# Two early stages of the third mixer in two parts each, other gate arithmetic, fewer and other filler matmuls

## The chip, the cores and the metric

One NeuronCore of a Trainium2 chip runs one program. The metric is the device time of one execution in microseconds. The engines are TensorE (PE, matmuls), VectorE (DVE), ScalarE (ACT), GpSimd (POOL) and the DMA queues that SyncE and ScalarE issue. Each engine works through its own list of instructions in order; semaphores join the lists.

## The reference, cut to what matters

Two layers of a decoder trunk, 512 prompt tokens and 8 sample tokens together (520 columns), width 1024. Each layer has four mixers that share one input projection, four gates, an output projection and a gated feed-forward part:

```python
h = _rmsnorm(x, p['norm_mix_w']) * (1.0 + sc1) + sh1
proj = (h @ p['w_in']).astype(f32)             # columns of the four mixers and of the gates
...
conv = jax.nn.silu(conv)                       # third mixer: 4-tap convolution over tokens
q = _l2norm(_heads(conv[..., :o1], GDN_H)) * HEAD_DIM ** -0.5
k = _l2norm(_heads(conv[..., o1:o2], GDN_H))
g_log = -jnp.exp(p['gdn_a_log']) * jax.nn.softplus(Pg[..., a_off:a_off + GDN_H] + p['gdn_dt_bias'])
beta = jax.nn.sigmoid(Pg[..., a_off + GDN_H:])
o, s_gdn = _gated_delta_chunked(q, k, v, g_log, beta, st_gdn.astype(f32))
...
gates = jax.nn.sigmoid(proj[..., OFF_GATE:])
for n, y_b in enumerate((y_rw, y_ret, y_gdn, y_hg)):
    term = gates[..., n * D_MODEL:(n + 1) * D_MODEL] * (y_b @ p['w_branch'][n])
    merged = term if merged is None else merged + term
out = merged.astype(h.dtype) @ p['w_out']
```

## The kernel before

All four engines walk the same list, made by `plan_layer()`. It interleaves two kinds of entries. The **mixer stages** `("mix", n, i)` are short steps of the recurrences, in the order HG, RW, GD, RT (HGRN2, RWKV-7, gated DeltaNet, retention): each mixer is a Python generator on each engine, and one `yield` ends one stage there. The **dense tasks** are the large products: `proj` (a 128-column tile of the input projection), `gate` (such a tile of a gate's projection, and then the branch product that it gates), `ada` and `turn` (the modulation). `IDLE`, made of the lists `BEFORE`, `PAIR` and `AFTER`, has one number per stage, and the dense tasks are shared out among the stages in proportion to it; its length is the number of stages.

On PE a dense task is a generator too. `operands()` of a stage first runs up to 30 matmuls of the current or next dense task (`fill`), then waits for the stage's operands. A dense entry of the plan makes PE finish that task (`finish`). Only one task beyond those due may be begun. A projection or gate tile is 48 matmuls at L803 (three for each of 8 slices of K and each half of the columns: the weights are split into a rounded part `w_hi` and a rest `ring_lo`); a gate adds four matmuls at L837. Results go to two banks of PSUM, `gm`, in turn. `bank()` waits until the bank's last content was taken: by ACT (L1585 copies a projection, L1594 takes the gate's sigmoid into `GT`, L1333 takes `ada`) or by DVE (L2274 and L2277 multiply branch product and gate, L2220 takes `turn`). Since these takers stand in the list at their place in the plan, a gate is taken only after all that ACT has in the stages before it.

`keep_busy(n)` issues n filler matmuls of constants (L767) whose result nobody reads. They are emitted only where a bank is open to write to. The numbers `AT_START`, `AT_TILE`, `AT_SAMPLES`, `AT_FFN_NORM`, `AT_END` and the arguments `busy=` say how many stand where. The trace shows every 4-byte matmul (L767, L931, L837) as two records, so 22 fillers are 44 records.

The rounding of a weight tile to `w_hi` is done by ACT (L1355) or by POOL (L732), by the set `on_scalar`; the rest `ring_lo` is made by POOL (L735). `early()` is the head of the GD mixer, run during RW: ACT makes six scaled copies of the projections (L1509), and DVE's generator `convolution()` adds the taps; `beside()` runs one or two of its steps inside the RW pair and chunk stages. A pair stage of RW on DVE (L2079 to L2085) calls `beside(2)` first, then takes PE's scores.

In GD the stages 0 and 1 hold, on PE, two sums over heads (L931 on `WK`) and two products of the gate parameters (L931 on `AB`); on ACT the sigmoid, logarithms and exponentials L1521 to L1529; on DVE L2111 to L2128. Stage 2 is the cumulative sum on DVE (L1768, L1774) and three exponentials on ACT (L1534 to L1536). Stage 3 makes the operands L2134 to L2138 on DVE and turns them over on PE (L942).

## Time and profile before

| | |
|---|---|
| Time, median of 3 runs | 2695.78 us (2693.8 to 2711.17) |
| Profiled execution, its time | 2704.68 us |
| Profiled execution, its span | 2702.9 us |
| Mean granted clock of TensorE | 0.928 |
| PE busy | 2361.5 us, 87% of the span |
| DVE, POOL and ACT busy | 1138.1, 844.8 and 731.2 us |
| DMA | 233.39 MB, 86 GB/s |

The span is what the trace covers; the profiled execution's own time is 1.8 us longer, and 8.9 us above the median. The granted clock is a share of TensorE's full speed of 2.4 GHz: 1.00 is 2.4 GHz and 0.50 is 1.2 GHz. The first layer's mixers run from about 45 to 860 us of the span, its feed-forward part to about 1370 us, and the second layer repeats this some 1330 us later.

### The profile page before, as it was taken

The page shows a single profiled execution, that of the slowest core. Times are in us where ns is not written, and L with a number is a line of the kernel's source. Part 1 is how long each engine was busy: PE and PEld are TensorE (multiplying, and loading weights), DVE is VectorE, ACT ScalarE, POOL GpSimd, SP SyncE. Part 2 cuts the span into 40 slices and gives each one's busy share as a digit, 9 for nine tenths or more (in the row PEclk, how much of TensorE's full clock was granted, in tenths as well). Part 3 has the DMA queues.
Part 4 walks back from the last instruction along what each step waited for, and adds up shares of the span by engine and source line. Part 5 has one row for each costly group of instructions (what it writes and reads, how often), then busy time and mean ns, then how long its engine had stood idle before and what let it go on. Part 6 is the DMA issues. An engine that isn't in the chain of part 4 may idle for free. (4 is left out here: it accounts for less than half of the span.)

```text
span 2702.9 us, 46568 instructions
## 1 busy us (share of the span) xinstructions
PE 2361.5 (87%) x20592; PEld 2176.8 (81%) x20592; DVE 1138.1 (42%) x1558; ACT 731.2 (27%) x915; POOL 844.8 (31%) x602
## 2 busy tenths in 40 slices
PE   5878978689899989999977789777898899999997
PEld 3767866578778979999976679656787699999997
DVE  5164464555444532221233546655734445222212
ACT  2432311322212232222224333104222133322222
POOL 2311210133133434444432213101322234444442
PEclk8988988889999999999988989778999999999998
DMA  6331121111232324322233311111112322222222
GB/s 250 118 110 57 60 72 46 45 51 45 80 102 87 117 88 127 120 91 87 94 120 117 105 54 59 61 55 48 52 52 73 115 77 102 79 94 94 87 93 73
DMA packets 68457, 233.39 MB, mean 86 GB/s; under 512 B 10784, under 2 KB 11296, under 8 KB 67872
## 3 DMA queue, kind: packets, MB, share of 16 engines
q1 hardware_dynamic: 61344, 214.88, 24.1%
q10 hardware_dynamic: 6912, 15.53, 1.6%
q8 instruction: 162, 2.65, 0.4%
q14 instruction: 39, 0.32, 0.0%
HBM read 219.03 MB, written 11.35 MB: 85 GB/s over the span
## 5 line engine op out<-in xcount | busy, mean ns | idle before, releaser
L735 POOL TENSOR_TENSOR ring_lo<-ring,w_hi 128x512 fp32r<-128x512 f32 x552 | 769.9, 1416 | 1429.8 <-ACT w_hi L1355 1361.2
L803 PE MATMUL gm<-H_hi,ring_lo 128*128 128x260 f32 x3456 | 749.2, 299 | 98.1 <-ACT GT L1594 34.1
L803 PE MATMUL gm<-H_hi,w_hi 128*128 128x260 f32 x3456 | 720.9, 290 | 0.0
L803 PE MATMUL gm<-H_lo,w_hi 128*128 128x260 f32 x3456 | 719.9, 291 | 0.0
L803 PEld LDWEIGHTS gm<-H_hi,ring_lo 128*128 128x128 f32 x3456 | 559.6, 197 | 142.5 <-ACT GT L1594 39.9
L803 PEld LDWEIGHTS gm<-H_lo,w_hi 128*128 128x128 f32 x3456 | 554.2, 196 | 2.3 <-issue 1.9
L803 PEld LDWEIGHTS gm<-H_hi,w_hi 128*128 128x128 f32 x3456 | 553.7, 195 | 1.6 <-issue 0.8
L1355 ACT ACTIVATE w_hi<-ring 128x1024 fp32r<-128x1024 f32 x268 | 282.9, 1056 | 447.4 <-PE gm L803 186.0
L752 POOL TENSOR_TENSOR X<-X,GT 128x520 f32<-128x520 f32 x32 | 49.8, 1557 | 323.6 <-DVE GT L2277 323.6
L1279 PE MATMUL gm<-AF_hi,ring_lo 128*128 128x260 f32 x704 | 142.1, 283 | 3.3 <-DVE AF_lo L2301 3.3
L1279 PE MATMUL gm<-AF_hi,w_hi 128*128 128x260 f32 x704 | 141.5, 282 | 0.0
L1279 PE MATMUL gm<-AF_lo,w_hi 128*128 128x260 f32 x704 | 141.3, 282 | 0.0
L2306 DVE TENSOR_TENSOR AT<-gm,GT 128x520 f32<-128x520 f32 x44 | 30.8, 700 | 253.0 <-ACT GT L1635 253.0
L2235 DVE TENSOR_SCALAR Y<-gm,MOD 128x520 f32<-128x520 f32 x32 | 24.3, 759 | 258.0 <-PE gm L1279 217.1
L1594 ACT ACTIVATE GT<-gm 128x520 f32<-128x520 f32 x64 | 38.6, 603 | 343.7 <-PE gm L803 316.5
L837 PE MATMUL gm<-Y,WB 128*128 128x260 f32 x512 | 123.6, 384 | 0.0
L1279 PEld LDWEIGHTS gm<-AF_hi,ring_lo 128*128 128x128 f32 x704 | 108.3, 188 | 3.7 <-DVE AF_lo L2301 3.7
L1279 PEld LDWEIGHTS gm<-AF_lo,w_hi 128*128 128x128 f32 x704 | 108.6, 188 | 0.0
L1279 PEld LDWEIGHTS gm<-AF_hi,w_hi 128*128 128x128 f32 x704 | 108.3, 188 | 0.0
L767 PE MATMUL gm<-CN 128*128 128x128 f32 x652 | 86.9, 296 | 21.6 <-ACT PJ L1585 13.5
L767 PEld LDWEIGHTS gm<-CN 128*128 128x128 f32 x652 | 83.7, 210 | 24.4 <-ACT PJ L1585 15.5
L837 PEld LDWEIGHTS gm<-Y,WB 128*128 128x128 f32 x512 | 93.4, 191 | 11.6
(410 smaller groups left out, 2750.4 us busy)
## 6 DMA issues: line engine op xcount, KB each, us to landing
ring<-wall SPq DMA_DIRECT2D x372, 512.0 KB, 3.3
WB<-wbranch SPq DMA_DIRECT2D x32, 256.0 KB, 3.6
xsave<-X SPq DMA_DIRECT2D x2, 2080.0 KB, 12.1
X<-xsave ACTq DMA_DIRECT2D x8, 520.0 KB, 5.3
arena<-states ACTq DMA_DIRECT2D x8, 512.0 KB, 3.4
sst<-arena ACTq DMA_DIRECT2D x8, 512.0 KB, 3.7
X<-xt SPq DMA_DIRECT2D x1, 2080.0 KB, 12.1
y<-H SPq DMA_DIRECT2D x4, 520.0 KB, 2.7
```

Of the source, the lines that this page charges most:

```text
L735: pool.tensor_tensor(ring_lo[:, SLOT[i], k], ring[:, SLOT[i], k], hi[:, k].bitcast(F32), ALU.subtract).then_inc(parts_ready, 1)
L752: pool.tensor_tensor(MG[:, m, :], MG[:, m, :], GT[:, :], ALU.add).then_inc(gate_used, 1)
L767: pe.matmul(out, cst("blocks"), cst("ident"), start=False, stop=False, skip_group_check=True)
L803: ins = pe.matmul(out[:, hf, 0:HALF], w[a][:, k, :], src[b][:, k, HALF * hf:HALF * (hf + 1)], start=first and a == "lo", stop=last and a == b)
L837: ins = pe.matmul(out[:, hf, 0:HALF], WB[:, m // 2 % 2, m % 2, k, :], Y[:, k, HALF * hf:HALF * (hf + 1)], start=k == 0, stop=k == 1)
L1279: ins = pe.matmul(out[:, hf, 0:HALF], w[a][:, i % 8, :], AF_parts[b][:, f, HALF * hf:HALF * (hf + 1)], start=f == 0 and a == "lo", stop=f ...
L1355: act.activation(w_hi[:, j % 2], ring[:, SLOT[splits[j][0]]], ACT.Copy).then_inc(hi_made, 1)
L1594: act.activation(h2(GT[:, :]), src, ACT.Sigmoid).then_inc(done, 1)
L2235: step(ts(h2(WR), src, MOD[:, at + m, 0:1], None, MUL))
L2306: taken(tt(h2(AT[:, f % 2, :]), src, h2(GT[:, :]), MUL), done)
```

## The change

There are seven edits.

1. **GD stages in two.** `BEFORE[GD]` has two entries more, and each engine's generator has its `yield`s to match. Old stage 0 (both head sums, with all of L1521 to L1529 on ACT) becomes stages 0 and 1, with gate task RW 0 between them in the plan; old stages 1 and 2 move to 2 and 3, and old stage 2's exponentials on ACT go to stage 4, behind gate task RW 2.
2. **Gate arithmetic.** ACT takes tanh(x/2) where it took the sigmoid. DVE computes (tanh + 1) times the product in one instruction, and the factor 0.5 goes into the split of the merged sum.
3. **Convolution later.** `convolution()` begins with two empty steps, so the first `beside(2)` does nothing.
4. **Fillers at tiles.** `AT_TILE` and `AT_SAMPLES` have other numbers. In each layer 12 fillers fewer stand ahead of projection tile GD 2, 7 fewer at GD 5, 15 fewer at RT 1, 3 fewer at RT 6 and 2 fewer at gate GD 0; 5 more at gate RW 7, 8 more at HG's sample stage, 4 more at the start.
5. **Fillers ahead of a bank wait.** `AT_BANK` puts 18 fillers ahead of the waits of `ada` 18 and of projection RW 2 (`("proj", 1, 2)`), 12 ahead of that of projection GD 0; they write to the unused half of a bank (`half_only`).
6. **Feed-forward norm.** 18 fillers instead of 22 in the first layer, 26 in the second. The arguments `busy=21` and `busy=4` of RW's pair stages go; no bank is open at those places, and the instruction lists have no filler there before or after.
7. **Rounding moved.** With `BUSY` and `held_up`, nine tiles of each layer are rounded by POOL (L732) that were rounded by ACT (L1355).

```diff
-AT_START, AT_END, AT_FFN_NORM, AT_INNER = 14, 6, 22, 7
-AT_TILE = {("proj", 2, 2): 20, ("proj", 2, 5): 7, ("proj", 3, 1): 15, ("proj", 3, 6): 8, ("gate", 2, 0): 7}
-AT_SAMPLES = {0: (0, 0), 1: (22, 5), 2: (0, 5), 3: (2, 0)}
+AT_START, AT_END, AT_INNER, AT_SUMS, AT_FFN_NORM = 18, 6, 7, (0, 22), (18, 26)
+AT_TILE = {("proj", 2, 2): 8, ("proj", 3, 6): 5, ("gate", 2, 0): 5, ("gate", 1, 7): 5}
+AT_BANK = {("ada", 0, 18): 18, ("proj", 1, 2): 18, ("proj", 2, 0): 12}
+AT_SAMPLES = {0: (8, 0), 1: (22, 5), 2: (0, 5), 3: (0, 0)}
...
-          GD: [10, 10, 8, 8, 4] + [5] * DIAGONAL,
+          GD: [8, 2, 10, 4, 4, 8, 4] + [5] * DIAGONAL,
...
+BUSY = {(RW, 3), (RW, 4), (RW, 6), (GD, 1), (GD, 5), (GD, 7), (GD, len(BEFORE[GD])), (GD, len(BEFORE[GD]) + 6), (RT, 0)}
...
+            held_up = {j for j in range(3, mixing + 2)
+                       if any(kind == "mix" and (n, m) in BUSY for kind, n, m in plan[at[j - 3]:at[j - 2]])}
...
+                    if (kind, n, m) in AT_BANK and any(half_only):
+                        keep_busy(AT_BANK[kind, n, m], gm[:, half_only.index(True), 1, HALF:HALF + P128])
...
-                        act.activation(h2(GT[:, :]), src, ACT.Sigmoid).then_inc(done, 1)
+                        act.activation(h2(GT[:, :]), src, ACT.Tanh, scale=0.5).then_inc(done, 1)
...
                 def convolution():
 
+                    yield
+                    yield
                     from_scalar()
...
-                            taken(tt(h2(GT[:, :]), src, h2(GT[:, :]), MUL), done)
+                            taken(stt(h2(GT[:, :]), h2(GT[:, :]), 1.0, src, ADD, MUL), done)
```

**PE, start of GD.** The list from the last part of gate RW 0 to the second product of `AB` (L837 is the branch product of a gate, L931 on `arena` a head sum; a line of dots stands for further rows of the same tile). Before:

```order
L837 MATMUL gm<-Y,WB 128x260 x4
L931 MATMUL mx<-arena,CN 128x260 x4
L803 MATMUL gm<-H_hi,ring_lo 128x260 x2
...
L931 MATMUL mx<-AB,CN 128x260 x4
L803 MATMUL gm<-H_hi,ring_lo 128x260 x2
...
L837 MATMUL gm<-Y,WB 128x260 x4
L931 MATMUL mx<-AB,CN 128x260 x4
```

After (lines 808, 842 and 940 are 803, 837 and 931 of before):

```order
L842 MATMUL gm<-Y,WB 128x260 x4
L808 MATMUL gm<-H_hi,ring_lo 128x260 x2
...
L940 MATMUL mx<-arena,CN 128x260 x4
L808 MATMUL gm<-H_hi,ring_lo 128x260 x2
...
L842 MATMUL gm<-Y,WB 128x260 x4
L940 MATMUL mx<-AB,CN 128x260 x8
```

Thirty matmuls of gate RW 1 now stand ahead of the second head sum, and the other eighteen with its branch product behind it; between the two products of `AB` nothing stands any more, where before 18 matmuls and a branch product did.

**ACT, start of GD.** The same stretch (L1525 is the logarithm of a head sum, L1527 the exponentials, L1594 a gate, L1534 the exponentials of old stage 2). Before:

```order
L1525 ACTIVATE arena<-mx,CN 128x1040 x2
L1527 ACT_TABLE_LOAD
L1527 ACTIVATE arena<-arena 128x1040 x2
L1528 ACTIVATE arena<-arena 4x520
L1529 ACT_TABLE_LOAD
L1529 ACTIVATE arena<-arena,CN 4x520
L1594 ACT_TABLE_LOAD
L1594 ACTIVATE GT<-gm 128x520
...
L1534 ACT_TABLE_LOAD
L1534 ACTIVATE DI<-arena 128x16
```

After (L1535 is 1525, L1539 is 1527, L1541 is 1529, L1607 is 1594, L1547 is 1534):

```order
L1535 ACTIVATE arena<-mx,CN 128x1040
L1607 ACT_TABLE_LOAD
L1607 ACTIVATE GT<-gm 128x520
...
L1535 ACT_TABLE_LOAD
L1535 ACTIVATE arena<-mx,CN 128x1040
L1539 ACT_TABLE_LOAD
...
L1541 ACTIVATE arena<-arena,CN 4x520
L1607 ACT_TABLE_LOAD
L1607 ACTIVATE GT<-gm 128x520 x2
...
L1547 ACTIVATE DI<-arena 128x16
```

Gate RW 0 is taken between the two logarithms, gates RW 1 and RW 2 both before the exponentials of L1534, and those need no table load of their own. Over the program there are 68 table loads instead of 74; one new load in each layer stands ahead of L1514, the sigmoids of the convolution.

**DVE, first pair stage of RW.** Before:

```order
L1724 COPY CVO<-PJ 128x6x8
L1698 TENSOR_TENSOR CT<-CVI,PR 128x48 x2
...
L2079 TENSOR_TENSOR arena<-mx,CN 128x1024
L2080 TENSOR_TENSOR arena<-mx,CN 128x1024
L1709 SCALAR_TENSOR_TENSOR PJ<-PJ,PR 128x509
L1709 SCALAR_TENSOR_TENSOR PJ<-PJ,PR 128x510
L2084 TENSOR_TENSOR arena<-mx,CN 128x1024
```

After (L2094, L2095 and L2099 are 2079, 2080 and 2084; L1713 is 1698):

```order
L1739 COPY CVO<-PJ 128x6x8
L2094 TENSOR_TENSOR arena<-mx,CN 128x1024
L2095 TENSOR_TENSOR arena<-mx,CN 128x1024
L1713 TENSOR_TENSOR CT<-CVI,PR 128x48 x2
...
L1718 TENSOR_TENSOR arena<-arena,CT 128x2x8
L2099 TENSOR_TENSOR arena<-mx,CN 128x1024
```

The two scores are taken ahead of the convolution's first step, which waits for ACT's six copies; the last two additions of the convolution (L1709) now come behind L1908, after RW's sample stages.

## Rows read from the trace of the kernel before

**Rows 1.** The page, busy time by engine.

```profile
PE 2361.5 (87%) x20592; PEld 2176.8 (81%) x20592; DVE 1138.1 (42%) x1558; ACT 731.2 (27%) x915; POOL 844.8 (31%) x602
```

**Rows 2.** Who PE waited for: total us, times, longest us.

```profile
PE gm L803 <- ACT GT L1594: 34.1, 6, 9.4
...
PE mx L955 <- DVE arena L2080: 21.1, 4, 8.2
...
PE gm L803 <- DVE MT L2220: 14.3, 2, 7.2
...
PE gm L803 <- ACT PJ L1585: 10.0, 2, 5.0
```

**Rows 3.** Timeline, first pair stage of RW, first layer (start us, us).

```profile
376.30 0.19 DVE L1724 COPY CVO<-PJ 128x48 f32<-128x48 f32 x1
...
381.59 0.45 DVE L1698 TENSOR_TENSOR CT<-CVI,PR 128x48 f32<-128x48 f32 x2 [5.10 <-ACT arena L1509]
...
384.57 1.21 DVE L2080 TENSOR_TENSOR arena<-mx,CN 128x1024 f32<-128x1024 f32 x1
...
385.83 2.08 PE L955 MATMUL mx<-arena,PJ 64*128 64x128 f32 x16 [7.85 <-DVE arena L2080]
...
392.15 0.69 PE L998 MATMUL mx<-arena 32*32 32x32 f32 x32 [0.66 <-DVE arena L2085]
```

**Rows 4.** Timeline, start of GD, first layer.

```profile
518.83 2.02 PE L931 MATMUL mx<-arena,CN 128*128 128x260 f32 x8 [2.54 <-DVE arena L2112]
...
526.60 1.13 ACT L1525 ACTIVATE arena<-mx,CN 128x1040 f32<-128x1040 f32 x1 [2.19 <-PE mx L931]
527.74 1.28 ACT L1527 ACT_TABLE_LOAD   x1
529.04 2.17 ACT L1527 ACTIVATE arena<-arena 128x1040 f32<-128x1040 f32 x2
...
535.88 0.80 PE L803 MATMUL gm<-H_hi,ring_lo 128*128 128x260 f32 x2 [9.38 <-ACT GT L1594]
...
542.37 2.02 PE L931 MATMUL mx<-AB,CN 4*128 4x260 f32 x8
...
561.50 1.23 DVE L1774 TENSOR_TENSOR arena<-arena 128x1024 f32<-128x1024 f32 x1
...
567.11 0.80 PE L803 MATMUL gm<-H_hi,ring_lo 128*128 128x260 f32 x2 [7.38 <-ACT GT L1594]
...
568.09 2.21 DVE L2135 TENSOR_TENSOR arena<-PJ,arena 128x1024 f32<-128x1024 f32 x1
...
569.18 4.48 POOL L735 TENSOR_TENSOR ring_lo<-ring,w_hi 128x512 fp32r<-128x512 f32 x2
...
573.73 1.23 DVE L2138 TENSOR_TENSOR arena<-PJ,arena 128x1024 f32<-128x1024 f32 x1
```

**Rows 5.** Stretches: length; PE, PEld, DVE, ACT, POOL busy; granted clock; DMA.

```profile
536.00:542.00 6.00, 6.00 (x28) 6.00 (x29) 2.71 (x3) 0.78 (x1) 4.46 (x3) 0.51 0.01 3
...
567.00:572.00 5.00, 4.89 (x22) 4.89 (x23) 4.75 (x4) 1.01 (x2) 4.07 (x3) 0.50 0.00 0
...
239.00:245.00 6.00, 5.83 (x27) 5.84 (x28) 0.00 (x0) 2.34 (x3) 2.50 (x2) 0.50 0.06 11
```

**Rows 6.** Timeline, fillers of the first layer, by start.

```profile
290.81 1.83 PE L767 MATMUL gm<-CN 128*128 128x128 f32 x14 [1.00 <-ACT PJ L1585]
...
511.22 5.07 PE L767 MATMUL gm<-CN 128*128 128x128 f32 x44
...
626.83 5.24 PE L767 MATMUL gm<-CN 128*128 128x128 f32 x30 [2.48 <-DVE GT L2277]
...
628.09 2.50 POOL L735 TENSOR_TENSOR ring_lo<-ring,w_hi 128x512 fp32r<-128x512 f32 x2
```

**Rows 7.** POOL's groups by shape: count, busy us, mean ns.

```profile
L732 POOL TENSOR_TENSOR w_hi<-ring,CN 128x1024 fp32r<-128x1024 f32 x8 | 16.4, 2046 | 15.9 <-DMA ring<-wall 14.2 <-PE gm L803 1.7
```

**Rows 8.** Timeline, ACT at the end of RW, first layer.

```profile
497.69 2.17 ACT L1514 ACTIVATE PJ<-PJ 128x1040 f32<-128x1040 f32 x2 [24.06 <-issue]
```

More of the change, by code:

```diff
@@ L656, in build @@
                 room_after[i] = latest
-            on_scalar = {j for j, (i, _) in enumerate(splits)
-                         if j >= mixing + 2 and j - mixing - KT not in (0, 1) or (2 <= j < mixing + 2 and room_after[i] <= at[j - 2])}
+            held_up = {j for j in range(3, mixing + 2)
+                       if any(kind == "mix" and (n, m) in BUSY for kind, n, m in plan[at[j - 3]:at[j - 2]])}
+            on_scalar = {j for j, (i, _) in enumerate(splits) if j not in held_up
+                         and (j >= mixing + 2 and j - mixing - KT not in (0, 1)
+                              or (2 <= j < mixing + 2 and room_after[i] <= at[j - 2]))}
             rounds_after = {at[j - 2]: j in on_scalar for j in range(2, mixing + 2)}
@@ L847, in ada @@
                     out = bank()
+                    half_only[(used[1] - 1) % 2] = True
                     for k in range(0, KT // 2, 2):
@@ L863, in turn @@
                     out = bank()
+                    half_only[(used[1] - 1) % 2] = True
                     for h in range(2):
@@ L986, in diagonal_scores, with inverse @@
                     return ins
-                def inverse(cp, busy=0):
+                def inverse(cp):
                     def blocks():
@@ L994, in blocks @@
                                 yield u, u // 2 * NC + 2 * cp + u % 2, slice(a, a + BLK), slice(a + BLK, a + 2 * BLK)
-                    operands(FILL_SHORT, busy=busy)
+                    operands(FILL_SHORT)
                     for u, m, i, j in blocks():
@@ L1144, in rwkv @@
                         yield
-                        operands(busy=4 if cp else 21)
+                        operands()
                         scores(0, cp, pj(RW, 1), WK[:, 0])
@@ L1148, in rwkv @@
                         yield
-                        yield from inverse(cp, 4 if cp else 0)
+                        yield from inverse(cp)
                         for ci in range(2):
@@ L1256, in _ @@
                 coming(-1)
-                if layer + 1 == DEPTH:
-                    keep_busy(AT_FFN_NORM, mx[:, 3, 0:P128])
+                keep_busy(AT_SUMS[layer], mx[:, 3, 0:P128])
                 pe.wait_ge(operands_v, count.next(operands_v))
                 feature_sums()
-                keep_busy(AT_FFN_NORM, mx[:, 3, 0:P128])
+                keep_busy(AT_FFN_NORM[layer], mx[:, 3, 0:P128])
                 for m in range(2 * FT):
@@ L1593, in _ @@
                         gates += 1
-                        act.activation(h2(GT[:, :]), src, ACT.Sigmoid).then_inc(done, 1)
+                        act.activation(h2(GT[:, :]), src, ACT.Tanh, scale=0.5).then_inc(done, 1)
                         g[0] += 1
                         if n == RT and m:
-                            step(act.activation(MG_hi[:, m - 1, :], MG[:, m - 1, :], ACT.Copy), for_vector)
+                            step(act.activation(MG_hi[:, m - 1, :], MG[:, m - 1, :], ACT.Copy, scale=0.5), for_vector)
                     if x in rounds_after and rounds_after[x]:
@@ L1600, in _ @@
                 act.wait_ge(gate_used, gates)
-                step(act.activation(MG_hi[:, KT - 1, :], MG[:, KT - 1, :], ACT.Copy), for_vector)
+                step(act.activation(MG_hi[:, KT - 1, :], MG[:, KT - 1, :], ACT.Copy, scale=0.5), for_vector)
                 for k in range(0, KT, 2):
@@ L2114, in gdn @@
                     projected(GD)
+                    yield
                     from_scalar()
@@ L2228, in split_sum @@
                     from_scalar()
-                    step(tt(MG_lo[:, m, :], MG[:, m, :], MG_hi[:, m, :].bitcast(F32), SUB), x_ready)
+                    step(stt(MG_lo[:, m, :], MG[:, m, :], 0.5, MG_hi[:, m, :].bitcast(F32), MUL, SUB), x_ready)
                 def residual(m, at):
@@ L2273, in _ @@
                             dve.wait_ge(x_saved, 16)
-                            taken(tt(h2(MG[:, m, :]), src, h2(GT[:, :]), MUL), done)
+                            taken(stt(h2(MG[:, m, :]), h2(GT[:, :]), 1.0, src, ADD, MUL), done)
                             step(dve.tensor_copy(NA[:, :], NA[:, :]), gate_used)
                         else:
-                            taken(tt(h2(GT[:, :]), src, h2(GT[:, :]), MUL), done)
+                            taken(stt(h2(GT[:, :]), h2(GT[:, :]), 1.0, src, ADD, MUL), done)
                             if n == RT:
```

10 lines of the change are left out of this document (8 added, 2 removed).

## The prediction

> **What bounds the kernel now.** I read the page's busy times first: PE works 2361.5 of 2702.9 us [rows 1], no other engine half of it. So the 341 us in which PE stands, and the stretches at half clock, are what a change of order can win. The list of waits then says whom PE waits for [rows 2]: first for ACT taking a gate (34.1 us in 6 waits), and high up for DVE's L2080 (21.1 us in 4). The timeline shows the two large ones of each kind, once per layer. In GD's first stage PE stands 9.38 us until ACT, after two logarithms, the exponentials and their table loads, takes gate RW 0; behind the next stage it stands 7.38 us, since gate RW 1's successor is taken only after the exponentials of L1534 [rows 4]. In RW's first pair stage PE stands 7.85 us because DVE's L2079 and L2080 stand behind a convolution step that waits for ACT's copies [rows 3]. After such waits the granted clock is at its lower level for some us: 0.51 over 536 to 542, 0.50 over 567 to 572 [rows 5]. The reader is to see in each that the engine named did other work first: order, not speed, makes the wait.
>
> **The change part by part, for one layer.**
>
> *A, convolution later.* DVE is through with L1724 at 376.5, and PE's scores are there (PE ended them before it finished gate HG 4). L2079 and L2080, 1.2 us each, then end at 379.0 instead of 385.8 [rows 3]. PE goes on at 379.0 and needs 2.1 us at full clock for the scores. DVE's next pair, L2084 and L2085, stands behind the convolution's step, which ACT still releases at 381.6; its small products take 1.8 us, the pair 2.4: ready at 385.8. PE's L998 starts there at 392.15 [rows 3]. So of the 7.85 us, 6.3 are won, and a new wait of some 3 us ahead of L998 is what is late next. The two additions pushed behind RW's samples cost DVE 0.75 us each, once, ahead of the next head sum; PE had no wait there, so I put down 1.0. A: -6.3 + 1.0.
>
> *B, GD in two.* I follow the chain from 518.83, where PE starts the first head sum [rows 4]. ACT ends the first logarithm at 524.4 (its next wait, 2.19, begins there), loads a table (1.28), takes gate RW 0 at 526.3. PE, done with that gate at 524.8, waits 1.5 us where it waited 9.38, runs 30 matmuls of gate RW 1 (a fraction of the 48 of a tile, which take 5.8 us at full clock; 3.6), then the second head sum, to 532.0. ACT had the logarithm's input at 526.6 before and has it at 532.0 now: 5.4 us later. From there, 1.13 for the logarithm, 1.28, 2.17 and 0.64 for load and exponentials, 1.28 and 0.73 for the last logarithm: 539.2; DVE's two steps on `AB` end at 540.5. PE starts the first product of `AB` there, 1.8 us ahead of 542.37 [rows 4], after standing some 4 us. The second follows with only DVE's copy between (1.24): 544.0 where it was 550.0. From there to the end of L1774 it took 12.7 us before, so DVE ends at 556.8 instead of 562.7. Then ACT's exponentials (2.3) and, with gate RW 2 already taken, no table load, no gate and no further product on DVE ahead of L2134: 559.3 against 567.9. DVE's five steps to L2138 took 7.1 us, with POOL beside them (2.21 for L2135, against 1.23 for L2138 of the same size [rows 4]); I keep 6.5. PE turns them over at about 565.8 instead of 575.0: -9.2, and it can be -11 if POOL is elsewhere. PE has 11.3 us of dense work between 546 and there, so it stands about 7 us just ahead of L942, and the clock falls as it did. The cover of the chain is gone, the chain is the bound of this stretch; behind it the lists are alike. The bounds are 0 (the chain stays as long as it was) and -11. B: -9.2.
>
> *C, fillers.* 22 fillers, 44 records, take 5.07 us [rows 6]: 0.23 each at full clock. At GD 2 twelve go, but PE next waits for a chain of DVE (token shifts) that ends where PE arrives now: 0. At GD 5 the 7 take 1.83 and a wait for the tile's rest stands behind them, which POOL's own rounding removes: -2.4. At RT 1 the 15 take 5.24, partly at the lower clock [rows 6]; they start at 626.83, POOL's L735 for that tile starts at 628.09 and has its first half by 629.35, so PE goes on at 629.4 instead of 631.8: -2.4. The 3 and 2 others: -1.2. The 5 added at gate RW 7 lie in the 2.48 us ahead of 626.83: 0. C: -6.0.
>
> *D, fillers ahead of bank waits.* 18, 18 and 12 fillers are 4.1, 4.1 and 2.8 us; the waits are 6.5, 7.2 and 5.0, the last two standing in [rows 2] as two equal waits each (14.3 and 10.0). They are covered. What they can give is clock: PE worked 5.83 us of 239 to 245 at the lower level [rows 5], half of it is 2.9. Whether it is given I can't see; bounds 0 and -6 for the three places; I take -1.5.
>
> *E, table load at L1514.* ACT goes straight from a sigmoid gate to L1514 now [rows 8]; behind tanh a load of 1.28 stands in between, and what follows (gate HG 7, L2097 on DVE behind it, the next head sum) is a chain: +1.3. This trace has the next instruction right behind a load: 527.74 plus 1.28 is 529.02, and L1527 starts at 529.04 [rows 4]. The Trainium skill (ScalarE: Activation LUTs, "What ACT_TABLE_LOAD costs") adds a drain of 1380 ns to each switch; by it E would be +2.7 and the whole 3 us later, and the trace doesn't bear it out.
>
> *F, rounding on POOL.* 2.05 us a tile [rows 7] against 1.05 on ACT. POOL is busy 31% of the span [rows 1] and the tile is needed a dense task (5.8 us) later: covered. Not free is its company: L2135 takes 1.0 longer beside POOL [rows 4]. One of the nine in DVE's bound stretch: +1.0; bounds 0 and the rival's. DVE's fused gate product against a plain one: equal in the trace's instructions of this shape within 0.1, and DVE isn't the bound at most of them: 0. Fillers at the start, at HG's samples and at the norms stand ahead of waits as long as they: 0.
>
> **Sum.** -5.3 - 9.2 - 6.0 - 1.5 + 1.3 + 1.0 = -19.7 a layer; the second layer's waits are the first's within 0.4 us ([rows 2] has them in pairs), so -39.4. The profiled execution would take 2704.7 - 39.4 = 2665.3; it lies 8.9 above the median of the three, so the median becomes 2656.4. I say **2657**.
>
> **The rivals.**
>
> *R1, the clock pays for the fillers.* 39 fillers of each layer go where they followed a wait, and B leaves waits of 4 and 7 us. For it: every long wait here ends in a stretch at 0.5 [rows 5]. Against: fillers behind a wait run at the low clock themselves, and real matmuls follow at once. One more fall costs half of 4.9 us; at four places a layer, 8 times 2.4 is 19.6: 2676. The Trainium skill (TensorE: Matmul & The Clock Gate, Part 1) says that the default state is throttled and activity releases it; by it the order of filler and work doesn't matter, but the idle time does, and that speaks for this rival at B's waits.
>
> *R2, the split gives back.* The second head sum stands behind 30 matmuls, and a chain that is cut has more hand-overs. If the chain after the second product of `AB` doesn't shorten as I have it, only the 1.8 us of the first product are left: 7.4 less a layer, 2672. That is also the case in which the change doesn't do what it says.
>
> *R3, slower: POOL's rounding.* A tile comes 1.0 us later by the longer rounding and 2.0 later where DVE's company stretches L735 (4.48 for the two beside L2135 [rows 4], 2.50 for two others [rows 6]), and DVE loses 2.05: 5.05 in all where both lie on the path. It decides from 8 of the 18 tiles, where 39.4 is used up; at 10 it is +50.5 and 2707. Against it: PE's waits for POOL are short, and DVE waits for others in most of the stages chosen.
>
> *R4, more.* The clock stays up where the waits shrink: at five places a layer half of some 4 us, 2 each, 20 in all: 2637.
>
> **How the numbers follow.** Forecast 0.48, R1 0.14, R2 0.17, R3 0.07, R4 0.14. The 27 us that are 1% of the median are about what a measurement can tell from no change; the border is 2668.8. The forecast's own spread (0 to -11 of B, 0 to -6 of D, twice) is 2640 to 2675, nine tenths below the border. Faster by over 1%: 0.43 and R4 0.14, a third of R2 and a fifth of R1, 0.66. Slower by over 1%: 0.06, most of R3. Within 1%: 0.28. The range leaves out R3 and the lower part of R4: 2634 to 2684.
>
> **What would show it.** Right: L2080's waits gone, 3 us ahead of L998; the 9.4 us wait at 1 to 2, 4 to 5 us ahead of the first product of `AB`, some 7 ahead of L942; L942 9 us earlier after the first head sum; 626.8's fillers gone with 2.5 us for POOL. Wrong: a mean granted clock below 0.92 (R1), L942 less than 4 us earlier (R2), waits of 3 us or more for `ring_lo` (R3). I would be most wrong if PE, freed at one place, only waits longer for DVE at the next, since these stretches are chains of DVE and ACT.

## The result and the profile after

The changed kernel took 2683.83 us (median of 8 runs, 2675.61 to 2688.24), the kernel before 2702.12 beside it (8 runs): a ratio of 0.9928, interval 0.9906 to 0.9949, or 19.5 us less where 39.4 were forecast. The 2683.83 stand against 2657 and lie at the upper end of the range, 2684. The spans of the two profiled executions, 2702.9 and 2679.4 us, differ by 23.5. On the median of 2695.78 that the prediction started from, the ratio gives 2676.4.

Line numbers moved (x9, x11, x12, x13 and x17 add two more to those of ACT and DVE): L803 is L808 now, L767 is L772, L931 is L940, L942 is L951, L955 is L964, L998 is L1007, L732 and L735 are L737 and L740, L1514 is L1524, L1768 is L1783. Page of the changed kernel, busy time [rows 1], and then its waits of PE [rows 2]:

```profile
PE 2371.0 (88%) x20696; PEld 2188.1 (82%) x20696; DVE 1140.4 (43%) x1558; ACT 706.7 (26%) x891; POOL 880.6 (33%) x620
```

```profile
PE mx L1083 <- DVE arena L1911: 21.3, 8, 6.6
PE gm L808 <- POOL ring_lo L740: 20.9, 10, 5.2
...
PE mx L951 <- DVE arena L2155: 14.5, 2, 7.6
...
PE mx L1007 <- DVE arena L2100: 10.2, 4, 2.6
...
PE mx L940 <- DVE AB L2137: 9.6, 2, 4.8
```

The two waits that the change was aimed at are gone from the head of the list: 34.1 us for ACT's gates and 21.1 us for L2080 [rows 2]. In their place stand waits that were not there: 4.8 us ahead of each first product of `AB`, about 7 ahead of each turning L951, 2.6 ahead of L1007, and 5.2 for `ring_lo`. The timeline of PE shows where they lie. First RW's first pair stage, where 392.15 stood in [rows 3]:

```profile
378.46 0.98 PE L1007 MATMUL mx<-arena 32*32 32x32 f32 x32 [2.60 <-DVE arena L2100]
```

Then the start of GD [rows 4], dense matmuls left out:

```profile
505.27 3.52 PE L940 MATMUL mx<-arena,CN 128*128 128x260 f32 x8 [2.32 <-DVE arena L2127]
516.96 1.92 PE L940 MATMUL mx<-arena,CN 128*128 128x260 f32 x8
527.59 3.83 PE L940 MATMUL mx<-AB,CN 4*128 4x260 f32 x8 [4.82 <-DVE AB L2137]
532.82 3.83 PE L940 MATMUL mx<-AB,CN 4*128 4x260 f32 x8 [1.40 <-DVE arena L2139]
557.45 3.68 PE L951 MATMUL mx<-CN,arena 128*128 128x128 f32 x16 [6.90 <-DVE arena L2155]
```

The reader is to look at the second column, the time an instruction group took. A product over `AB` takes 3.83 us, and took 2.02 in [rows 4]; the turning takes 3.68, and took 1.97 in the kernel before. The windows say why (length, busy us of PE, PEld, DVE, ACT, POOL, granted clock, DMA):

```profile
526.00:530.00 4.00, 2.41 (x6) 1.90 (x7) 1.18 (x3) 2.12 (x3) 0.00 (x0) 0.50 0.00 0
530.00:534.00 4.00, 2.60 (x7) 1.56 (x6) 1.24 (x1) 0.00 (x0) 0.00 (x0) 0.50 0.00 0
534.00:538.00 4.00, 4.00 (x13) 2.93 (x12) 1.24 (x1) 0.00 (x0) 0.00 (x0) 0.50 0.02 4
...
553.00:557.00 4.00, 0.00 (x0) 0.00 (x0) 3.90 (x4) 0.00 (x0) 0.58 (x1) 0.50 0.00 0
557.00:561.00 4.00, 3.55 (x17) 3.55 (x18) 0.40 (x1) 0.00 (x0) 0.00 (x0) 0.50 0.00 0
```

PE idles just ahead of the product that the chain needs, the granted clock is at its lower level (1.2 GHz) by then, and the product itself pays. In the kernel before the lower clock fell on dense matmuls behind the wait [rows 5]; the products over `AB` and L942 came after them, at 2.4 GHz. That is the point that the prediction missed.

**A ruler for GD.** I cut the stretch into five legs by the starts of PE's products: first head sum, first and second product over `AB`, turning L951 (L942 before), first product of the diagonal (L1195), first product of its inverse (L1212). In us, first layer / second layer:

| kernel | sum to AB 1 | AB 1 to AB 2 | AB 2 to turning | turning to diagonal | diagonal to inverse |
|---|---|---|---|---|---|
| before | 23.54 / 23.42 | 7.63 / 7.62 | 25.01 / 25.04 | 9.27 / 9.27 | 36.04 / 36.00 |
| changed | 22.32 / 21.90 | 5.23 / 5.23 | 24.63 / 24.63 | 11.88 / 11.20 | 37.45 / 37.48 |
| changed, a second profile (x16) | 21.87 / 21.89 | 5.23 / 5.24 | 24.63 / 24.64 | 12.02 / 11.11 | 39.48 / 37.46 |
| split alone (x2) | 21.88 / 21.88 | 5.23 / 5.23 | 23.04 / 23.04 | 11.49 / 11.58 | 36.05 / 36.00 |
| ACT rounds (x3) | 21.90 / 21.87 | 5.23 / 5.23 | 23.03 / 23.00 | 11.98 / 11.90 | 35.82 / 35.87 |
| RW's tiles on POOL (x10) | 21.90 / 22.17 | 5.24 / 5.23 | 23.01 / 23.01 | 11.14 / 11.55 | 35.81 / 35.82 |
| cover at turning (x4) | 21.90 / 22.35 | 5.23 / 5.23 | 24.62 / 24.66 | 9.28 / 9.28 | 37.51 / 37.48 |
| cover at AB (x9) | 21.89 / 21.90 | 3.88 / 3.42 | 24.62 / 24.63 | 11.02 / 11.85 | 37.46 / 37.46 |
| both covers and x10 (x11) | 21.87 / 21.90 | 3.42 / 3.42 | 23.04 / 23.03 | 9.28 / 9.29 | 37.18 / 36.09 |
| sum first (x5) | 18.92 / 18.43 | 9.83 / 10.01 | 22.79 / 22.78 | 10.65 / 10.73 | 39.45 / 39.45 |
| x11 and sum first (x12) | 18.44 / 18.44 | 3.80 / 3.66 | 26.38 / 26.39 | 9.27 / 9.27 | 37.26 / 35.94 |
| and the gate whole (x17) | 18.79 / 18.79 | 3.42 / 3.42 | 23.02 / 23.04 | 9.29 / 9.27 | 37.52 / 35.80 |

The first three legs repeat within 0.5 us from one profile to the next, the third within 0.03, the fourth within 0.9, the last within 2.0. A ratio of times has an interval of about 0.0025 to each side, some 7 us. So I read these stretches by the legs, and by the ratio only whether the whole follows.

**A ruler for the rest.** For the other stretches I took the start of the same DVE instruction in two traces and followed the difference. HG's own stretch (161 to 346 us of the kernel before) doesn't repeat: the changed kernel gained 7.8 us there in its first profile and 4.8 in the second, x16. The same 10 us of both, from 190 on, first profile then second:

```profile
190.00:200.00 10.00, 6.64 (x48) 3.75 (x42) 4.70 (x9) 3.22 (x5) 2.54 (x2) 0.89 0.40 150
```

```profile
190.00:200.00 10.00, 8.73 (x40) 5.11 (x40) 3.89 (x9) 1.99 (x4) 2.54 (x2) 0.57 0.30 107
```

One program, and the clock there is 0.89 in one execution and 0.57 in the other. A difference of a few us in such a stretch between two single profiles isn't an effect.

### The profile page after: what moved, and what is told of

Its sections match the earlier page's. It is cut to its first block and busy times, and to the rows that moved or that the text cites. A ratio compares the mean times of both kernels' runs of the same rounds, so it can differ in the third digit from the quotient of the medians.

```text
span 2679.4 us, 46752 instructions
## 1 busy us (share of the span) xinstructions
PE 2371.0 (88%) x20696; PEld 2188.1 (82%) x20696; DVE 1140.4 (43%) x1558; ACT 706.7 (26%) x891; POOL 880.6 (33%) x620
## 3 DMA queue, kind: packets, MB, share of 16 engines
HBM read 219.03 MB, written 11.35 MB: 86 GB/s over the span
## 5 line engine op out<-in xcount | busy, mean ns | idle before, releaser
L740 POOL TENSOR_TENSOR ring_lo<-ring,w_hi 128x512 fp32r<-128x512 f32 x552 | 769.9, 1415 | 1332.2 <-ACT w_hi L1365 1301.0
L808 PE MATMUL gm<-H_hi,ring_lo 128*128 128x260 f32 x3456 | 748.6, 298 | 61.6 <-POOL ring_lo L740 20.9
L808 PE MATMUL gm<-H_lo,w_hi 128*128 128x260 f32 x3456 | 717.2, 290 | 0.0
L808 PE MATMUL gm<-H_hi,w_hi 128*128 128x260 f32 x3456 | 717.1, 289 | 0.0
L808 PEld LDWEIGHTS gm<-H_hi,ring_lo 128*128 128x128 f32 x3456 | 558.1, 196 | 102.2 <-issue 23.5
L808 PEld LDWEIGHTS gm<-H_lo,w_hi 128*128 128x128 f32 x3456 | 552.4, 195 | 0.9 <-issue 0.5
L808 PEld LDWEIGHTS gm<-H_hi,w_hi 128*128 128x128 f32 x3456 | 550.6, 194 | 1.3 <-issue 0.5
L1365 ACT ACTIVATE w_hi<-ring 128x1024 fp32r<-128x1024 f32 x250 | 264.0, 1056 | 449.2 <-PE gm L808 186.0
L757 POOL TENSOR_TENSOR X<-X,GT 128x520 f32<-128x520 f32 x32 | 48.8, 1525 | 313.7 <-DVE GT L2294 313.7
L1607 ACT ACTIVATE GT<-gm 128x520 f32<-128x520 f32 x64 | 38.6, 603 | 371.7 <-PE gm L808 338.5
L772 PEld LDWEIGHTS gm<-CN 128*128 128x128 f32 x756 | 96.0, 208 | 21.3 <-ACT PJ L1598 13.4
L772 PE MATMUL gm<-CN 128*128 128x128 f32 x756 | 99.7, 293 | 15.0 <-ACT PJ L1598 11.8
## 6 DMA issues: line engine op xcount, KB each, us to landing
X<-xt SPq DMA_DIRECT2D x1, 2080.0 KB, 12.1
```

The source lines that it names most:

```text
L740: pool.tensor_tensor(ring_lo[:, SLOT[i], k], ring[:, SLOT[i], k], hi[:, k].bitcast(F32), ALU.subtract).then_inc(parts_ready, 1)
L757: pool.tensor_tensor(MG[:, m, :], MG[:, m, :], GT[:, :], ALU.add).then_inc(gate_used, 1)
L772: pe.matmul(out, cst("blocks"), cst("ident"), start=False, stop=False, skip_group_check=True)
L808: ins = pe.matmul(out[:, hf, 0:HALF], w[a][:, k, :], src[b][:, k, HALF * hf:HALF * (hf + 1)], start=first and a == "lo", stop=last and a == b)
L1365: act.activation(w_hi[:, j % 2], ring[:, SLOT[splits[j][0]]], ACT.Copy).then_inc(hi_made, 1)
L1607: act.activation(h2(GT[:, :]), src, ACT.Tanh, scale=0.5).then_inc(done, 1)
```

## The experiments

Ratios are to the kernel before, timed on the same chip, with 95% intervals.

**x1, part A alone.**

```diff
                 def convolution():
 
+                    yield
+                    yield
                     from_scalar()
```

> The kernel before with the convolution's two empty stages alone (part A). Forecast's term: -5.3 a layer, -10.6 in all, ratio to the kernel before 0.9961; the trace of the whole change shows the interval around L998 shorter by 6.5 a layer, which would be -13 and 0.9952. Rival: PE only waits longer later, for the head sum that stands behind the two moved additions: 0, ratio 1.000.

0.9938 [0.9915, 0.996], span 10.7 us shorter. By the starts of DVE's instructions it gains 5.8 us from 371 to 396 us in the first layer and 6.3 at the same place in the second, and has lost nothing of it by the head sum of GD. So the rival, that PE only waits longer later, doesn't hold, and the 1.0 that I charged for the two additions isn't there. By the times it is 16.8 us, between 11 and 23, which is more than the trace shows; the two agree in kind, and the size rests on one profile.

**x2, part B alone.**

```diff
-          GD: [10, 10, 8, 8, 4] + [5] * DIAGONAL,
+          GD: [8, 2, 10, 4, 4, 8, 4] + [5] * DIAGONAL,
...
                     head_sums(WK[:, 0]).then_inc(mix_done_a, 1)
+                    yield
                     operands(sem=operands_a)
```

> The kernel before with GD's two stages cut alone (part B); sigmoid gates, fillers and all roundings stay as they were. Read: the time from PE's first head sum of GD to its turning of L942, 56.2 us in the kernel before and 52.2 in the changed one. If my forecast's B held and only the company of the other parts spoiled it: 47, and -18 in all, 0.993. If POOL's moved roundings took the difference: 50.5, -11 to -14, 0.995. If the cut itself gives no more, since PE's products of the chain run at the lower clock behind bare waits: 52 and -4 a layer, -8, 0.997.

0.9988 [0.9965, 1.0011], span 3.1 shorter. Sum to turning 50.2 us, between my cases; but turning to diagonal is 2.2 and 2.3 longer than before, so 3.8 us are left in one layer and 3.6 in the other. PE of this kernel (its L942 is the turning):

```profile
541.62 3.83 PE L931 MATMUL mx<-AB,CN 4*128 4x260 f32 x8 [4.82 <-DVE AB L2127]
546.85 3.83 PE L931 MATMUL mx<-AB,CN 4*128 4x260 f32 x8 [1.40 <-DVE arena L2129]
569.89 3.61 PE L942 MATMUL mx<-CN,arena 128*128 128x128 f32 x16 [5.43 <-DVE arena L2145]
```

All three products run at half clock though no filler was removed and no rounding moved. The slow products come with the split itself. The times alone couldn't tell this gain from none; the legs do.

**x3 and x10, who rounds.** x3 takes `held_up` out of `on_scalar`, so that ACT rounds all nine tiles a layer again; x10 keeps POOL for three of the nine stages.

```diff
 x3
-            on_scalar = {j for j, (i, _) in enumerate(splits) if j not in held_up
+            on_scalar = {j for j, (i, _) in enumerate(splits) if j not in ()
 x10
-BUSY = {(RW, 3), (RW, 4), (RW, 6), (GD, 1), (GD, 5), (GD, 7), (GD, len(BEFORE[GD])), (GD, len(BEFORE[GD]) + 6), (RT, 0)}
+BUSY = {(RW, 3), (RW, 4), (RW, 6)}
```

> The changed kernel with all of the nine moved tiles a layer rounded on ACT again. If POOL's rounding beside DVE costs what the two traces show (scans of L1783 7.43 us for 5.75, diagonal inverse 34.9 for 33.3): -3.3 a layer, -6.6, ratio to the kernel before 0.9904, and the eight scans at 5.8. If it costs nothing, because the roundings on ACT then stand in ACT's chain with 1.05 us each: 0 to +4, ratio 0.993 to 0.9945.

> The changed kernel with POOL's rounding kept only for the tiles under RW's stages, and ACT's again under GD and RT. All on ACT gave 0.9899; its trace gains 3.5 us in GD and 2.6 in RT a layer on the changed kernel and loses some 3 a layer just ahead of RW. If those losses are the price of ACT's rounding there, this kernel has both gains and not the loss: 6 us a layer less than the changed kernel, ratio 0.9885. If the loss is a play of the clock: as all on ACT, 0.990.

0.9899 [0.9873, 0.9926] and 0.9883 [0.9863, 0.9904]. In both, the third leg is 1.6 us and the last 1.6 shorter than in the changed kernel, in both layers: 3.2 a layer. The instructions behind this, changed kernel first (DVE, then POOL), x10's same steps of DVE after it:

```profile
540.35 7.43 DVE L1783 TENSOR_TENSOR_SCAN arena<-CN,arena 128x128 f32<-128x128 f32 x8
...
592.82 1.60 DVE L1819 TENSOR_TENSOR arena<-arena 128x450 f32<-128x450 f32 x1
...
595.11 1.76 DVE L1823 TENSOR_SCALAR arena<-arena,HALVES 128x128 f32<-128x128 f32 x2
```

```profile
541.83 2.01 POOL L737 TENSOR_TENSOR w_hi<-ring,CN 128x1024 fp32r<-128x1024 f32 x1
...
591.72 2.21 POOL L737 TENSOR_TENSOR w_hi<-ring,CN 128x1024 fp32r<-128x1024 f32 x1
```

```profile
538.04 5.79 DVE L1783 TENSOR_TENSOR_SCAN arena<-CN,arena 128x128 f32<-128x128 f32 x8
...
588.13 0.99 DVE L1819 TENSOR_TENSOR arena<-arena 128x450 f32<-128x450 f32 x1
...
589.82 0.74 DVE L1823 TENSOR_SCALAR arena<-arena,HALVES 128x128 f32<-128x128 f32 x2
```

The scans take 1.64 us longer, L1819 and L1823 together 1.63 longer. The instructions one by one say how. Here are one scan of the changed kernel, the instructions of POOL behind its second rounding, and eight scans of the kernel before during which POOL stands until the last one:

```profile
542.07 2.04 DVE L1783 TENSOR_TENSOR_SCAN arena<-CN,arena 128x128 f32<-128x128 f32 x1
...
594.01 2.77 POOL L740 TENSOR_TENSOR ring_lo<-ring,w_hi 128x512 fp32r<-128x512 f32 x2
```

```profile
314.25 2.63 DVE L1768 TENSOR_TENSOR_SCAN arena<-CN,arena 128x128 f32<-128x128 f32 x8
```

A scan with nothing beside it takes 0.39 us. In x10 three of the eight take 1.4 each, beside three instructions that POOL has there in any case; in the changed kernel the rounding is a fourth, and the scan beside it takes 2.04, which is 1.65 more than 0.39. At the diagonal L1819 runs beside the rounding itself, 0.61 longer; one of the two L1823 takes 1.32 for 0.27 beside the second L740, which the rounding has pushed back to there. The Trainium skill (SBUF — State Buffer, "SBUF: two separate sides") has it that GpSimd and an instruction of VectorE with two inputs in SBUF share a pair of ports, that the first to start holds them for its whole instruction, and that the other is blocked. By the scans the trace agrees: one of 0.39 us takes 2.04 beside an operation of 2.01. Whether POOL's rounding under RW's stages, which x10 keeps, is worth something against x3 stays open: the ratios' intervals overlap.

**x4 and x9, cover for the waits.** x4 puts 26 fillers ahead of the turning, x9 16 ahead of the first product over `AB`. In x9 ACT signals its second logarithm to PE, since the fillers write a bank that ACT reads until then.

```diff
 x4
-                    operands()
+                    operands(busy=26)
                     to_tokens(0, WK[:, 2])
 x9
+                    operands(sem=operands_a)
+                    keep_busy(16, mx[:, 3, HALF:HALF + P128])
-                    operands()
+                    operands(0)
                     over_pair(lambda t: CN[0:4, ...
```

> The changed kernel with 26 fillers (6 us at full clock) ahead of the turning L951 of the changed kernel (L942 before), where PE stands 6.9 us. If the lower clock costs on the chain there: L951 takes 2.1 us instead of 3.8 and the way from it to the diagonal inverse's first product 9.3 instead of 11.9, up to 4 us a layer, 8 in all, ratio 0.990. If that way is longer for DVE's and POOL's sake: 1.7 a layer or nothing, 0.9915 to 0.993.

> The changed kernel with 16 fillers (3.7 us at full clock) put into the 4.8 us in which PE stands ahead of the first product of AB; they start once ACT has taken the second logarithm. If the lower clock behind the bare wait is what took B's gain: both products take about 2.0 us instead of 3.83, 3.6 us less to L942 on each layer, ratio to the kernel before 0.9928 less 0.0027, 0.990. If the clock is not raised by 3.7 us of fillers, or what follows waits anyway for DVE: 0 to +1, 0.993.

x4: 0.9905 [0.9883, 0.9927]. Its PE at the turning, and the clock where the changed kernel had 0.50:

```profile
549.14 5.97 PE L772 MATMUL gm<-CN 128*128 128x128 f32 x52
556.86 1.97 PE L951 MATMUL mx<-CN,arena 128*128 128x128 f32 x16 [1.75 <-DVE arena L2155]
```

```profile
553.00:557.00 4.00, 2.25 (x20) 2.06 (x20) 3.70 (x4) 0.00 (x0) 0.00 (x1) 1.00 0.00 0
557.00:561.00 4.00, 4.00 (x35) 4.00 (x35) 2.03 (x2) 0.00 (x0) 0.00 (x0) 1.00 0.02 4
```

Turning to diagonal is 9.28 in both layers, as in the kernel before to 0.01, and 1.9 to 2.6 shorter than in the changed kernel. x9: 0.9915 [0.9892, 0.9939]. The first product over `AB` takes 2.48 us in one layer and 2.02 in the other, the second still 3.83 behind the 1.40 that PE waits for DVE's copy. AB 1 to AB 2 is 1.35 and 1.81 shorter; the rest of what I expected there stays with the second product. No run put fillers ahead of that one.

**x5, the second head sum first.** `operands(sem=operands_a)` becomes `operands(0, sem=operands_a)`.

> The changed kernel with the second head sum of GD ahead of the 30 matmuls of gate RW 1, right behind ACT's release. ACT gets it 3.5 us earlier, and from there to AB all is a chain of ACT and DVE: if that chain is the bound, L951 comes 3.5 us earlier a layer, -7 in all, ratio 0.990. If PE only stands longer at the lower clock behind it (the 30 matmuls are the last dense work before AB, and they keep their place behind the sum): 0, 0.993.

0.9922 [0.9899, 0.9945]. The first leg is 3.4 shorter, the second 4.6 longer: PE now runs the gate's last 18 matmuls and its branch product between the two products, from 528.6 to 534.6 us, most of them at the lower clock. The third leg is 1.8 shorter, so the turning comes 0.6 us earlier after the head sum in the first layer and 0.5 in the second (0.2 against the first layer of x16), where 3.5 were looked for, and the last leg is 2.0 longer, which it is in one layer of x16 too. The earlier start was there and was given back between the products. One row of this run prices the second product over `AB`:

```profile
534.62 2.02 PE L940 MATMUL mx<-AB,CN 4*128 4x260 f32 x8
```

With dense work ahead of it this product takes 2.02 us instead of 3.83, and the leg that begins with it, up to the turning, is shorter by the same 1.8.

**x7, fillers ahead of bank waits taken out.** `AT_BANK = {}`.

> The changed kernel without the 18, 18 and 12 fillers ahead of waits for a bank (part D). The two traces drift apart by 10 us in layer 0 and 5.4 in layer 1 over the stretches of HG, where I had put down 1.5 a layer. If these fillers bring that by keeping the clock up: +10 to +12 in all, ratio to the kernel before 0.997. If it comes from other edits (fillers at the samples and the start, gates): +1 to +3, 0.994, and the offset at the first turning of RW stays near -7.

0.9934 [0.991, 0.9958]. Its HG stretch of the first layer gained 0.5 us on the kernel before where the two profiles of the changed kernel gained 7.8 and 4.8; in the second layer's it gained 5.1, they 3.4 and 3.9. The ratio is 1.6 us from the changed kernel's. By the profile the fillers bring 4 to 7 us in one layer and nothing in the other, by the times nothing that can be told. The other traces add to it. In the first layer's HG stretch all fifteen kernels with these fillers gained on the kernel before, 3.5 to 10.0 us, and the three without (x1, x2, x7) 0.3 to 1.5. Part of it has a place: between the DVE instructions at 238 and 253 us of the kernel before, just behind the 12 fillers of projection GD 0, the fifteen gain 1.0 to 2.6 us and the three lose or gain less than 0.3. In the second layer's HG stretch the fifteen lie between 5.5 gained and 2.8 lost, the three between 5.1 gained and 3.0 lost, so nothing can be told there. That the fillers gain in the first layer is likely by this; how much isn't settled, since the profiled execution of x7 was 6 us slower than its median.

**x6, x14, x15, fillers at tiles put back.** x6 has `AT_TILE` as before; x14 only the 15 at RT 1, x15 only GD 2's and GD 5's. x16 is the changed kernel itself beside the last two.

```diff
 x6
-AT_TILE = {("proj", 2, 2): 8, ("proj", 3, 6): 5, ("gate", 2, 0): 5, ("gate", 1, 7): 5}
+AT_TILE = {("proj", 2, 2): 20, ("proj", 2, 5): 7, ("proj", 3, 1): 15, ("proj", 3, 6): 8, ("gate", 2, 0): 7}
```

> The changed kernel with the fillers at tiles as they were before (part C undone). Forecast's term: +6 a layer, +12, ratio to the kernel before 0.997. By the changed kernel's trace the 15 fillers of RT 1 gave nothing, since PE waits 5.16 us for ring_lo in their place and the way to L1007 stays 11.8 us; what is left is GD 5 and the small ones, +2 to +3 a layer at most: 0.9935 to 0.995.

> The changed kernel with the 15 fillers at RT 1 back, nothing else. If they hold the clock over RT's first pair stage, as the trace with all fillers back shows (2.35 and 2.0 us less a layer around there): -4.4 us in all, 0.0016 less than the changed kernel beside it, 0.9912 if that is 0.9928. If they only delay, as I forecast: 4.8 more, 0.9946.

> The changed kernel with the fillers of GD 2 (20 for 8) and GD 5 (7 for 0) back, nothing else. Forecast: +2.4 a layer for GD 5's, 0 for GD 2's, 0.9946. By the trace with all back: over that stretch the way from 267 to 329 us is as long with as without, 2.1 us longer than before in each, so 0 and the changed kernel's ratio. If these carry the rest of the 12 us: 0.990.

> The changed kernel once more, beside the others and the kernel before. By the first comparison: 0.9928, within 0.9906 to 0.9949. Its trace tells how much one stretch of HG's mixer (150 to 260 us) varies between two executions of the same code: by the other kernels, which have the same code there, up to 6 us.

x6: 0.9883 [0.9862, 0.9904]; x14: 0.9895 [0.9869, 0.9921]; x15: 0.9926 [0.9899, 0.9953]; x16: 0.9919 [0.989, 0.9948]. No kernel with fillers back is slower by what part C was to save, and x6 is 12 us faster than the first comparison of the changed kernel and 10 faster than x16, which none of the forecasts had. The intervals of x14 and x16, timed side by side, overlap. RT 1 in the changed kernel:

```profile
612.55 0.70 DVE L2294 SCALAR_TENSOR_TENSOR GT<-GT,gm 128x520 f32<-128x520 f32 x1
613.28 2.16 DVE L2180 TENSOR_SCALAR arena<-mx,GC 128x128 f32<-128x128 f32 x8
613.33 1.28 POOL L757 TENSOR_TENSOR X<-X,GT 128x520 f32<-128x520 f32 x1 [9.10 <-DVE GT L2294]
614.57 2.50 POOL L740 TENSOR_TENSOR ring_lo<-ring,w_hi 128x512 fp32r<-128x512 f32 x2
615.98 0.77 PE L808 MATMUL gm<-H_hi,ring_lo 128*128 128x260 f32 x2 [5.16 <-POOL ring_lo L740]
...
618.63 2.08 PE L964 MATMUL mx<-PJ 64*128 64x128 f32 x16
...
624.32 0.69 PE L1007 MATMUL mx<-arena 32*32 32x32 f32 x32 [0.91 <-DVE arena L2187]
```

and PE in x6, with the fillers:

```profile
610.99 3.51 PE L772 MATMUL gm<-CN 128*128 128x128 f32 x30
615.75 1.16 PE L964 MATMUL mx<-PJ 64*128 64x128 f32 x16
616.74 1.06 PE L964 MATMUL mx<-arena,PJ 64*128 64x128 f32 x16
620.33 0.69 PE L1007 MATMUL mx<-arena 32*32 32x32 f32 x32 [0.90 <-DVE arena L2187]
```

and the same place in x16, which is the changed kernel again:

```profile
615.19 0.70 DVE L2294 SCALAR_TENSOR_TENSOR GT<-GT,gm 128x520 f32<-128x520 f32 x1
...
620.86 1.16 PE L964 MATMUL mx<-PJ 64*128 64x128 f32 x16 [0.69 <-DVE arena L2183]
...
625.44 0.69 PE L1007 MATMUL mx<-arena 32*32 32x32 f32 x32 [0.88 <-DVE arena L2187]
```

From DVE's L2294 to L1007 it was 11.83 us in the kernel before, with the 15 fillers. In the changed kernel it is 11.77: L964 runs at half clock (2.08 for 1.16) and takes up what the missing fillers gave. In x16's first layer the clock stayed up, L964 took 1.16, and the way was 10.25, the 1.6 us shorter that the edit could win. All traces together, two layers each: in the six kernels with the fillers L964 ran at full clock every time and the way took 10.25 to 11.83 us, 11.35 in the mean; in the thirteen without them it ran at full clock once in 26, and the way took 10.25 to 12.40, 11.56 in the mean. So the 15 fillers paid for themselves there through the clock. That place doesn't explain 6 to 12 us in the times of x6 and x14.

**x8, sigmoid gates and plain products again.** L1607 and the products of L2294 and its neighbours as in the kernel before.

> The changed kernel with sigmoid gates and plain products (part E undone). Forecast's term: ACT goes without a load from the gate to L1524, -1.3 a layer, -2.6, ratio to the kernel before 0.992. Rival: tanh shares a table with the exponentials, so sigmoid adds loads at other places of ACT's chains in GD: +1 to +3 a layer, 0.994 to 0.995.

0.9912 [0.9891, 0.9933]. From L2095 to L2100 of DVE (lines of the kernel before), where ACT takes L1524, it is 1.2 and 1.3 us shorter than the changed kernel: the term of part E. The rival, 1 to 3 us a layer lost by more table loads, doesn't show: x8 has 78 loads where the changed kernel has 68, and isn't slower.

**x11, x13, x12, x17, what adds up.** x11 is x10 with both covers (20 fillers at the turning); x13 adds all fillers of x6; x12 is x11 with the second head sum first and no fill between the products over `AB`; x17 changes one line more:

```diff
-                    operands(sem=operands_a)
+                    operands(2 * FILL, sem=operands_a)
                     keep_busy(16, mx[:, 3, HALF:HALF + P128])
```

> The changed kernel with POOL's rounding under RW's stages alone, 16 fillers ahead of the first product of AB and 20 ahead of the turning L951 (the three edits tried singly before). If they add up: on the kernel with the RW roundings alone (0.9883) another 1.35 us a layer at AB and 2.3 behind L951, 7 us in all, ratio 0.9857. If one cover's clock is only had once (PE's state at L951 doesn't depend on it, but what follows waits for DVE): 0.987 to 0.988.

> The kernel with both covers and POOL's rounding under RW's stages alone (0.9863), with all of the fillers at tiles as they were before. If the gain of 4.4 us at RT 1 is there too: 0.9847; if all 12 us of fillers back add up: 0.982; if the forecast's part C were right for this kernel: 0.989.

> As the kernel with both covers and RW's roundings alone, and besides the second head sum ahead of the 30 matmuls and none between the two products of AB. With the sum first alone PE reached the first product of AB 2.8 us after less than before but ran matmuls at the lower clock for 6 us between the two products. If those took the gain: the turning L951 3 us earlier a layer and 6 in all, ratio 0.9835. If the chain behind AB is bound by DVE and POOL in any case: 0.9857, as without it.

> The kernel with covers, RW's roundings and the second head sum first, and now up to 60 steps of dense work ahead of AB, so that gate RW 1 is whole before its first product. If DVE's wait of 3.13 us for this gate took the gain: head sum to AB 18.5 to 19 us, third leg 23.0 again, turning 3 us earlier a layer than in the other two, 6 in all, ratio 0.984. If the third leg stays at 26.4: 0.9865, and the chain there is bound by something else.

x11: 0.9863 [0.9839, 0.9887], the first four legs of x4, x9 and x10 in one kernel; the last leg is 1.4 longer than x10's in the first layer. x13: 0.9866 [0.9839, 0.9894], nothing more, so x6's 12 us don't add up here. In its second layer the cover at the turning failed, with the same 20 fillers as in x11:

```profile
1879.83 3.11 PE L951 MATMUL mx<-CN,arena 128*128 128x128 f32 x16 [2.19 <-DVE arena L2157]
```

The fillers ended 2.19 us ahead of the turning, where it was 0.71 in x11's first layer; the clock fell to 0.57 over 1880 to 1884, and the way from the turning to the diagonal took 10.9 us instead of 9.28. x12: 0.9868 [0.9845, 0.9892]: the first leg 3.4 shorter, the third 3.35 longer. Its DVE says why:

```profile
538.90 0.70 DVE L2296 SCALAR_TENSOR_TENSOR GT<-GT,gm 128x520 f32<-128x520 f32 x1 [3.13 <-ACT GT L1609]
539.64 5.80 DVE L1785 TENSOR_TENSOR_SCAN arena<-CN,arena 128x128 f32<-128x128 f32 x8
```

The gate product stands ahead of the scans and waits for a gate whose last 18 matmuls PE runs behind `AB` at the lower clock. x17 lets PE end that gate first: third leg 23.0, first 18.79, 0.9841 [0.981, 0.9871], as expected (0.984). Its median is 2660.27 us beside 2703.54 of the kernel before. PE in x17:

```profile
529.06 3.73 PE L772 MATMUL mx<-CN 128*128 128x128 f32 x32
532.72 2.02 PE L940 MATMUL mx<-AB,CN 4*128 4x260 f32 x8
```

## Why the prediction was half right

- **A, -5.3 a layer: right in kind, a little small.** x1 gives 5.4 a layer by its span, 5.8 and 6.3 by the trace and 8.4 by the times (5 to 12), with no sign of the +1.0. The new wait ahead of L1007 is 2.60, forecast 3.
- **B, -9.2: the step that failed is the price of the clock at B's waits, put at nothing.** x2 has -3.8 and -3.6. By legs, first layer: sum to `AB` -1.7 (forecast -1.8); `AB` 1 to 2 -2.4 (forecast 3.5 for 7.6, -4.1; the product is 1.8 longer); to the turning -2.0 (forecast -3.2, again a product 1.8 longer); turning to diagonal +2.2 (forecast 0). I wrote that PE "stands about 7 us just ahead of L942, and the clock falls as it did", and the wait came much as written, 5.4 us in x2's first layer and 6.9 to 8.3 in the two profiles of the changed kernel (by the forecast's own times, 565.8 less 546.0 less 11.3, it would be 8.5). Its price was taken as nothing because the fall itself was nothing new. What was new is the work behind it: a product of the chain instead of dense matmuls. By the two products at 3.83 for 2.02 and by the fourth leg, the clock costs 5.8 us a layer. x4, x5 and x9 show it, a term each: with PE kept busy the turning takes 1.97 and the fourth leg is that of the kernel before (x4), the second product over `AB` takes 2.02 and its leg is 1.8 shorter (x5), and the first takes 2.02 to 2.48 and its leg is 1.4 to 1.8 shorter (x9). Added up this is what x2 lacks, 5.4 and 5.6 us a layer, to 0.4 us.
- **R1 had the mechanism, at the wrong price.** It named the clock at B's waits, and called it one more fall worth 2.4 us. Near its 2676 the ratio did end, mostly through B, with F beside it; at RT 1 it was right on the fillers too. Its sign, a mean granted clock below 0.92, didn't come (0.934, and 0.928 before): a mean over the span doesn't show where the clock falls on the chain. R2 named the size of B's shortfall (L951 4.0 us earlier after the head sum in the changed kernel) without the cause: the chain wasn't longer in DVE or ACT. The Trainium skill (TensorE: Matmul & The Clock Gate, Part 1), by which throttled is the default and activity releases it, would have been the better guide to B: the trace agrees, with 0.50 at the end of waits of 4.8 and 6.9 us and 1.00 where fillers stood. R3's sign did come, a wait of 5.16 us for `ring_lo`, but it stands at RT 1 where the fillers stood, and the roundings cost 3.2 us a layer by x3 and x10.
- **C, -6.0: wrong, it gave nothing.** At RT 1 PE did go on 2.4 us earlier, 3.4 us after DVE's L2294 (615.98 against 612.55), and the next step that counts, L1007, came no earlier: L964 ran at the lower clock in between, a price that the forecast put at nothing here as well. At GD 5 the 2.4 us are won at 302 us of the kernel before, and 2.7 had been lost from 267 to 290, where L940 ran at the lower clock behind a wait (2.62 us for the 2.02 of the kernel before):

```profile
268.12 2.62 PE L940 MATMUL mx<-PJ,LO 128*128 128x260 f32 x8 [2.34 <-ACT PJ L1470]
```

  With the fillers back (x6, x15) the first of these stretches loses 1.0 and 1.3 us, the second gains 0.8, and the whole way from 267 to 302 is as long. So the 12 fillers taken at GD 2, forecast at 0, cost about what the 7 at GD 5 gave (x7, without them too, lost only 1.1 in the first stretch). The times of x6 and x14 say that taking fillers costs 6 to 12 us; those of x13 and x15 don't, and it stays open.
- **D, -1.5: not told apart by the times.** By the traces the fillers gain in the first layer, with a size between 2 and 10 us, and nothing can be told in the second.
- **E, +1.3: right**, 1.2 and 1.3.
- **F, +1.0: mis-sized, 3.2.** I charged the company of one rounding in DVE's bound stretch. Two of them lie there, at the scans and at the diagonal's last steps, and each cost 1.6, the second partly through the `ring_lo` steps that it pushed back.

In spans, over two layers: A -12.1, B -7.4, E +2.5, F +6.4, C nothing, sum -10.6, where the profiles differ by 23.5. The other 13 are mostly in HG's stretches (-7.8 and -3.4), which vary by clock; x16's profile has -4.8 and -3.9 there. By the traces compared under x7, 2 to 10 us of it may be D's; how much is play stays open. The range had a slip too: B from 0 to -11 and D from 0 to -6, twice each, give 2644 to 2678 and not 2640 to 2675.
